# The first of the 31 convolution taps of each channel chunk, made by ScalarE instead of VectorE

## What is computed

```python
h = x @ w_in                      # w_in: 1024 x 3072
q, f_pre, i_v, g, a, a_gate = split(h)
# HGRN2 heads: f = lb + (1-lb)*sigmoid(f_pre), log_f, chunked scan over q, k, i_v, gate g
u = a * jax.nn.sigmoid(a_gate)    # 256 tokens x 512 channels
u = lax.conv_general_dilated(     # depthwise, causal, CV_K = 31 taps
    u, cv_w, window_strides=(1,), padding=[(CV_K - 1, 0)],
    dimension_numbers=('NWC', 'WIO', 'NWC'), feature_group_count=CV_CH) + cv_b
u = jax.nn.silu(layer_norm(u, cv_ln_g, cv_ln_b))
y = jnp.concatenate([o, u], axis=-1) @ w_out
```

## Time and profile before

| What | Value |
|---|---|
| median of 3 runs | 1262.03 us (1262.0 to 1263.36) |
| time of the profiled execution | 1261.95 us |
| its span | 1260.1 us |
| TensorE busy | 1251.1 us, 99% of the span |
| VectorE busy | 826.4 us, 66% |
| ScalarE busy | 660.4 us, 52% |
| 120 taps of L1799 | 50.1 us busy, 588.5 to 669.4 us |

### The profile page before, as it was taken

One profiled execution on the slowest core, in us unless ns is written; L12 is line 12 of the kernel. 1 busy time (PEld: TensorE's weight loads), 2 busy tenths in 40 slices (PEclk: granted clock), 3 DMA queues, 4 the chain that ended last, 5 costly groups with the idle time before them and its releaser, 6 DMA issues.

```text
span 1260.1 us, 16736 instructions
## 1 busy us (share of the span) xinstructions
PE 1251.1 (99%) x6592; PEld 1074.7 (85%) x6592; DVE 826.4 (66%) x1268; ACT 660.4 (52%) x999; POOL 28.7 (2%) x33
## 2 busy tenths in 40 slices
PE   9999999999999999999999999999999999999998
PEld 8888888888888888899899997888888998888886
DVE  6655666878667665677999665755557665755554
ACT  7544546668574444454526645644445654644443
POOL 0000000010000000000000000000001000000000
PEclk9999999999999999999999999999999999999999
DMA  9655555552355555554434643655555442656552
GB/s 346 220 179 182 191 185 188 164 183 84 117 178 185 193 188 184 185 168 149 145 107 157 211 131 127 231 190 192 184 186 165 168 151 91 227 184 199 185 185 66
DMA packets 62572, 218.94 MB, mean 174 GB/s; under 512 B 6688, under 2 KB 10016, under 8 KB 61984
## 3 DMA queue, kind: packets, MB, share of 16 engines
q1 hardware_dynamic: 62352, 217.63, 52.2%
q10 hardware_dynamic: 144, 0.26, 0.1%
HBM read 216.81 MB, written 1.05 MB: 173 GB/s over the span
## 4 chain that ended last, share of the span: by engine, by line
PE 96%; DVE 2%; ACT 1%; issue 0%; DMA 0%; DVEq 0%; POOL 0%; ACTq 0%; POOLq 0%
PE bank L1977 27%; PE bank L1979 27%; PE bank L1978 27%; PE bank L1999 3%; PE bank L2201 2%; PE bank L2348 1%; PE bank L2309 1%; DVE arena L1799 1%; PE bank L2320 1%; PE bank L2412 1%; DVE w_lo L1158 1%; PE bank L2341 0%; PE bank L2303 0%; PE bank L2098 0%; PE bank L2065 0%
## 5 line engine op out<-in xcount | busy, mean ns | idle before, releaser
L1158 DVE TENSOR_TENSOR w_lo<-w_raw,w_hi 128x1024 fp32r<-128x1024 f32 x382 | 466.3, 1225 | 333.0 <-ACT w_hi L617 331.1
L617 ACT ACTIVATE w_hi<-w_raw 128x1024 fp32r<-128x1024 f32 x382 | 403.4, 1059 | 446.6 <-PE bank L1979 428.9
L1977 PE MATMUL bank<-w_hi,x_hi 128*128 128x512 f32 (+2 forms) x912 | 353.8, 388 | 0.4 <-DVE x_lo L1180 0.4
L1979 PE MATMUL bank<-w_hi,x_lo 128*128 128x512 f32 (+2 forms) x912 | 349.6, 383 | 0.0
L1978 PE MATMUL bank<-w_lo,x_hi 128*128 128x512 f32 (+2 forms) x912 | 349.4, 383 | 0.0
L1979 PEld LDWEIGHTS bank<-w_hi,x_lo 128*128 128x128 f32 x912 | 171.4, 188 | 33.3
L1977 PEld LDWEIGHTS bank<-w_hi,x_hi 128*128 128x128 f32 x912 | 171.5, 188 | 32.7 <-DVE x_lo L1180 0.7
L1978 PEld LDWEIGHTS bank<-w_lo,x_hi 128*128 128x128 f32 x912 | 171.5, 188 | 32.1
L1977 PE MATMUL bank<-w_hi,h_hi 128*128 128x512 f32 (+1 forms) x364 | 142.4, 391 | 0.0
L1979 PE MATMUL bank<-w_hi,h_lo 128*128 128x512 f32 (+1 forms) x364 | 141.3, 388 | 0.0
L1978 PE MATMUL bank<-w_lo,h_hi 128*128 128x512 f32 (+1 forms) x364 | 141.2, 388 | 0.0
(11 more groups left out here) (323 smaller groups left out, 1372.6 us busy)
## 6 DMA issues: line engine op xcount, KB each, us to landing
w_raw<-weights_d SPq DMA_DIRECT2D x394, 512.0 KB, 3.3
arena<-weights_d SPq DMA_DIRECT2D x4, 512.0 KB, 6.5
arena<-ln_rows_d SPq DMA_DIRECT2D x2, 1024.0 KB, 6.3
arena<-late_d SPq DMA_DIRECT2D x1, 1056.0 KB, 5.6
xs<-x_d SPq DMA_DIRECT2D x2, 512.0 KB, 7.5
kv_mem<-mem_d SPq DMA_DIRECT2D x1, 1024.0 KB, 9.4
out_d<-xs SPq DMA_DIRECT2D x4, 256.0 KB, 2.3
arena<-xT_d SPq DMA_DIRECT2D x3, 256.0 KB, 6.5
```

Of the source, the lines that this page charges most:

```text
L617: nc.scalar.activation(w_hi[:, slot(b), :], w_raw[:, b % RAW, :], ACT.Copy).then_inc(hi_ready, 1)
L1158: nc.vector.tensor_tensor(w_lo[:, slot(b), :], w_raw[:, b % RAW, :], w_hi[:, slot(b), :].bitcast(F32), ALU.subtract).then_inc(lo_ready, 1)
L1977: nc.tensor.matmul(out, wh, xh, start=start, stop=False, skip_group_check=True)
L1979: return nc.tensor.matmul(out, wl, xh, start=False, stop=stop, skip_group_check=True)
```

## The change

Tap 0 leaves VectorE's list. ScalarE makes it as an activation Identity with the tap's weight column as scale and `cv_b` as bias, at n = 2, 4, 6 and 8, right behind its `blk()`, and first waits there for `u_ready` of the chunk. It signals `tap_first`, for which VectorE's tap 1 of each chunk waits. The numbers in `beside` stay; `taps` starts at 1 for each chunk, and `comes` is (0, 12, 20, 30). To free a semaphore, the two signals of `dv_evac` are counted on `diff_evac`.

```diff
@@ scalar, loop over n
                 if n < 8 and n % 2:
                     done(b)
                     nc.scalar.activation(ag[:, n // 2, :], half(4 + n % 4, 0), ACT.Sigmoid).then_inc(ag_sig, 1)
+                if n in (2, 4, 6, 8):
+                    c = n // 2 - 1
+                    act.wait_ge(u_ready, c + 1)
+                    nc.scalar.activation(conv[:, c, :], ub[:, c, 0:S], ACT.Identity, scale=col("cv_w", c * CV_K),
+                                         bias=col("cv_b", c)).then_inc(tap_first, 1)
                 if 8 <= n < 12:
@@ vector
-            taps, made, comes = [0] * CC, [0] * CC, (0, 9, 17, 27)
+            taps, made, comes = [1] * CC, [0] * CC, (0, 12, 20, 30)
...
                     src, w = ub[:, c, k:k + S], col("cv_w", c * CV_K + k)
-                    if k == 0:
-                        dve.wait_ge(u_ready, c + 1)
-                        ins = nc.vector.tensor_scalar(conv[:, c, :], src, w, col("cv_b", c), ALU.mult, ALU.add)
+                    if k == 1:
+                        dve.wait_ge(tap_first, c + 1)
                     else:
                         dve.wait_ge(vec_chain, made[c])
-                        ins = nc.vector.scalar_tensor_tensor(conv[:, c, :], src, w, conv[:, c, :], ALU.mult, ALU.add)
+                    ins = nc.vector.scalar_tensor_tensor(conv[:, c, :], src, w, conv[:, c, :], ALU.mult, ALU.add)
@@ scalar and tensor: one semaphore for two
-                nc.scalar.activation(dv[:, t, :], PB[2 + t][:, :], ACT.Copy, scale=rs_tok[1][:, t:t + 1]).then_inc(dv_evac, 1)
+                nc.scalar.activation(dv[:, t, :], PB[2 + t][:, :], ACT.Copy, scale=rs_tok[1][:, t:t + 1]).then_inc(diff_evac, 1)
...
-            pe.wait_ge(diff_evac, 4)
-            pe.wait_ge(dv_evac, 2)
+            pe.wait_ge(diff_evac, 6)
```

More of the change, by code:

```diff
@@ L367, in build @@
             "res_ready xh_ready xl_ready y_ready na_ready nd_ready xn_ready xd_ready over_alpha")
-        proj_sq, var_ready, lat_norm, lat_t, lat_hi, lat_lo, v_up, vup_evac, dv_evac = sems(
-            "proj_sq var_ready lat_norm lat_t lat_hi lat_lo v_up vup_evac dv_evac")
+        proj_sq, var_ready, lat_norm, lat_t, lat_hi, lat_lo, v_up, vup_evac, tap_first = sems(
+            "proj_sq var_ready lat_norm lat_t lat_hi lat_lo v_up vup_evac tap_first")
         dq_sum, dq_n, dq_t, diff_evac, dk_n, dk_t = sems(
```

## The result

The changed kernel takes 1264.36 us (median of 20 runs, 1262.59 to 1266.61), the kernel before in the same session 1262.47 (20 runs, 1261.01 to 1263.68): a ratio of 1.0015, with a 95% interval of 1.0008 to 1.0021. So it is 1.9 us slower, and the interval leaves out 1. That is just inside the 0.2% that I called "no change", but the forecast was 1262.5 with an upper end of 1263.4: the loss is four times my 0.46 us, and the time lies outside the range.

What follows compares the result with a forecast made beforehand. TensorE, busy 1251.1 of 1260.1 us, was taken as the bound, with VectorE mattering only where TensorE waits; 0.09 before block 8 plus 0.37 at head 2 made 0.46 us more, so 1262.5 us, range 1261.1 to 1263.4.

Steps and rivals of the forecast that it cites:

- Head 2: VectorE's six taps behind head 2, now all chunk 3's, take 2.99 instead of 2.62 us: plus 0.37 on TensorE's wait.
- The rule of the Trainium skill: Dependent and alternating taps on VectorE would cost the same, so head 2 stays as it was; sum about 0.1 us.
- The runs before block 8: VectorE's two changed tap runs go from 2.93 to 3.00 and from 2.95 to 2.92 us: plus 0.07, minus 0.03.
- Four taps less behind head 3: VectorE's last run shrinks from six taps to two, 2.0 us less, but saves 0 on the path.
- ScalarE at n = 8: ScalarE waits for chunk 3's product and starts block 8's operations 2.7 us late, covered by some 5 us; cost 0.
- rival 3: ScalarE's lateness at n = 8 lasts until the scan, TensorE waits 2.1 to 2.7 us more, 1264.6 to 1265.2; 3%.
- No relief: TensorE's 0.9 us wait at block 8 for chunk 2's product is not relieved but grows to about 1.0.
- rival 1: ScalarE's tap relieves VectorE before block 8, up to 0.9 us gone: 1261.5, or 1261.1 without head 2's term; 6%.
- rival 2: Dependent taps on VectorE cost nothing extra, so head 2 is as long as before and the time 1262.1; 4%.
- Chunk 0's first tap: With the tap on ScalarE, VectorE goes on at 588.06 instead of 588.01: plus 0.05 us, bounds 0 and 0.09.

Runs made afterwards that it cites:

- e5: The changed kernel with chunk 0's first tap on ScalarE ahead of the high half of block 6 instead of behind it; 1263.30 us, ratio 1.0005.
- e7: The changed kernel with five extra dense products, results unused, on TensorE ahead of head 3's outputs; 1263.70 us, ratio 1.0015.
- e10: The changed kernel again, unaltered, as a control beside the last runs; 1264.02 us, ratio 1.0008.
- e11: The changed kernel with eight extra dense products between head 3's outputs and the one-column products; 1264.64 us, ratio 1.0019.
- e9: e8 with one block of memory products moved ahead of the one-column products and VectorE's two low halves ahead of head 3's taps; 1262.21 us, ratio 0.9995.
- e13: e9 with five taps each behind heads 2 and 3 and block 27's low half right behind the last taps; 1260.97 us, ratio 0.9985.
- e14: The kernel before with e13's orders on TensorE and VectorE, relief included, but no ScalarE tap and nine taps behind head 3; 1261.49 us, ratio 0.9994.
- e1: The changed kernel with four taps behind head 2 and four behind head 3, instead of six and two; 1262.79 us, ratio 1.0000.
- e6: e5 with four taps behind head 2 and four behind head 3, as in e1; 1262.22 us, ratio 0.9998.
- e4: The changed kernel with one tap less at n = 1 and n = 3, four behind head 2 and six behind head 3; 1262.56 us, ratio 0.9998.
- e8: e5 with e4's tables: five and six taps at n = 1 and 3, four behind head 2, six behind head 3; 1260.58 us, ratio 0.9991.
- e15: e8 again, unaltered, on the same chip as e13; 1260.71 us, ratio 0.9990.
- e2: The kernel before with seven taps behind head 2 and five behind head 3, instead of six and six; 1263.84 us, ratio 1.0011.
- e3: The kernel before with four taps behind head 2 and eight behind head 3, instead of six and six; 1263.32 us, ratio 1.0006.
- e12: The kernel before with its sixteen one-column products made twice; 1266.54 us, ratio 1.0032.

## Why the prediction was wrong

*Right, by its steps.* **Head 2:** I gave +0.37; 4.31 against 3.94 is +0.37, in each of the five profiles with that table (changed, e5, e7, e10, e11). Six dependent taps took 3.01, I had 2.99. The rule of the Trainium skill weighed there (VectorE: DVE Perf Modes, "The DRAIN you can't avoid") would have had them at 2.62; no run bears it out here. **The runs before block 8:** 3.00 and 2.90 us (588.46 to 591.46, 594.06 to 596.96), I had 3.00 and 2.92. **Four taps less behind head 3** saved nothing as long as nothing waited behind them. **ScalarE at n = 8:** 2.7 us late at most, level at block 10; rival 3 did not occur. **No relief:** rival 1 did not occur, and rival 2 neither.

*Wrong: "Chunk 0's first tap".* I took ScalarE's start at 586.43, after which the tap could come at 587.40, for a fixed point, with bounds of 0 and 0.09. But the instruction before the tap waits for a DMA, and 586.43 was one execution in which the weights were there. By executions the price at VectorE is 0 to 1.59 us. The high half before it, in the same profile of the kernel before, shows how large such a wait can be:

```profile
585.17 1.06 ACT L617 ACTIVATE w_hi<-w_raw 128x1024 fp32r<-128x1024 f32 x1 [2.77 <-DMA w_raw<-weights_d]
```

This row, not the overlap of two halves, should have set the upper bound. Mean price on stage 2–16: about 0.4 instead of 0.09.

*Missing: the granted clock.* No term of the sum had it: it stood at nothing. My one profile of before had the full clock, so nothing told me that nearly every second execution lost it behind head 3. One fall of 3.4 us costs 1.5 us; the changed kernel has them in 20 of 31 executions at least, against 57 of 121, and its mean clock is 0.9980 against 0.9986. Over 1262 us that is a difference of about 0.7. What the three runs of before did show was a spread of 1.4 us, one fall wide, and I used it for the range only.

*The sum by these:* 0.37 + 0.4 + 0.7 = 1.5 us. Measured on means, 2.0 (20 runs) and 1.2 (e10, 11 runs). The sizes of the last two terms are estimates from few profiles and from rounded clocks. Part of the sum can be had without profiles: executions at 1.000 had no fall behind head 3, and their medians are 1261.9 before (44) and 1262.6 changed (5). That is 0.7 without the clock, where 0.37 + 0.4 is 0.8.

*A sign with the wrong size.* I expected VectorE to be busy for 1.6 us less; it was 0.9 less (825.5 against 826.4). This says nothing about the path, and I did not follow it up.

*What stays open.* The fall's condition. Shown: twice the one-column products, always; a dense block of 2.9 us between head 3's outputs and them, never as far as the clocks tell (33 of 33 executions of e9, e13 and e14 at 0.999 or more, no fall there in their three profiles), though with VectorE's low halves moved as well; 0.6 or 1.0 us of dense products, no help. Not shown: why one execution of the same program falls and the next doesn't. e1 (1 of 11) and e6 (5 of 11) differ in the place of one tap alone, far from head 3, so counts out of eleven are too few to rank kernels that lie near each other. Put together they do say something on A in its weak form, that lateness makes falls more frequent. Where head 3's outputs came after 3.6 us and nothing waited behind them (e1, e4, e6, e8, e15), 19 of 55 executions were at 0.998 or below; at 3.9 (before) 57 of 121; at 4.3 to 4.5 (changed, e2, e5, e7, e11) 52 of 75. If the last group and the kernel before fell equally often, counts so far apart would have a probability of 0.003 (Fisher's exact test). The groups differ in other places too, and filling the wait (e7) changed nothing, so it is open what in the lateness does it, and how much of the 0.7 is due to it.

## What to carry to other kernels

When work moves to another engine, look at the instruction in front of its new place: if that one waits for a DMA, the consumer now waits for it too, in some executions only, so put the moved work ahead of it. When runs of a kernel spread more than the terms argued about, read the granted clock of many executions first, since one profile shows one draw. A stretch of small products is better broken up by a whole block of large ones than made shorter by tenths.

## What the runs showed of the hardware

The clock fell from 2.4 to 1.2 GHz though TensorE had waited for no more than 0.7 us at a time behind head 2, and in e6 and e8 for nobody. Ahead of each fall stood head 3's small work, at the full clock: the fall came behind the transposes (changed, e3, e4, e5), within them (e6), or already among the one-column products (e2, e8, e11, e12). It took 3.4 us (changed, e3 to e6, e11) or 6.8 (e2, e8, e12), and a dense product took 0.21 instead of 0.12 us in it. The Trainium skill says that matmuls should "execute back-to-back in batches", since the engine scales its power with utilization (Perfetto Trace Analysis, "Matmul Optimizations"); e12 against e13 agrees (granted clock 0.52 and 1.00 from 671 to 674 us), with the addition that here the clock fell behind small products that did follow each other back to back.

The busy columns show none of this: TensorE has 4.00 of 4.00 us from 668 to 672 in the changed kernel, in its small work, as in a dense block, and 1.00 of 1.00 at the lower clock.
